# Four attention items in flight and a new order of the early units in a two-layer NSA and HGRN2 decoder kernel

## The reference

```python
def reference(x, ...):
    for i in range(2):
        h = rms_norm(x, norm_w[i])
        y = nsa_mixer(h, ...) if i == 0 else hgrn2_mixer(h, ...)
        x = x + y
    return rms_norm(x, final_norm)

def nsa_mixer(h, w_in, ...):              # 16 heads of 64 in 4 groups
    q, kc, vc, ks, vs, kw, vw, gl, z = split_cols(h @ w_in, ...)
    v_cmp, k_cmp = compress(kv(vc), ...), rope(compress(kv(kc), ...), cmp_end)
    # compressed branch: 15 blocks of keys; selected and window branches: with
    # 256 tokens both see every causal key, each with its own K and V
    o = g0 * attend(q, k_cmp, v_cmp) + g1 * attend(q, ks, vs) + g2 * attend(q, kw, vw)
    return (o * jax.nn.silu(z)) @ w_out

def compress(kv, pe, w1, w2):             # blocks of 32 tokens, stride 16
    return jax.nn.silu((blocks(kv) + pe).reshape(...) @ w1) @ w2

def hgrn2_mixer(h, w_in, lb, g_norm, w_out):
    ...                                   # gated linear recurrence, 8 heads of 128
    return (norm(o) * g_norm * jax.nn.silu(z)) @ w_out
```

## Time and profile before

| what | us |
|---|---|
| median of 3 runs | 358.63 |
| lowest and highest run | 356.74, 360.58 |
| the profiled execution | 356.69 |
| its span, first to last instruction | 354.2 |
| PE busy in the span | 332.1 |
| DVE, ACT, POOL busy | 233.6, 181.8, 89.7 |

### The profile page before, as it was taken

How to read it: one execution, slowest core, us unless ns; L and a number is a source line. 1 busy time by engine, 2 the same in 40 slices (tenths; PEclk the granted TensorE clock), 3 DMA queues, 4 the chain that set the end, 5 groups by cost and what they waited for, 6 DMA issues and landing times.

```text
span 354.2 us, 5694 instructions
## 1 busy us (share of the span) xinstructions
PE 332.1 (94%) x2157; PEld 281.1 (79%) x2157; DVE 233.6 (66%) x396; ACT 181.8 (51%) x372; POOL 89.7 (25%) x83
## 2 busy tenths in 40 slices
PE   8999779999989969789899999999999999999993
PEld 5789577878979945466568878999999999889882
DVE  3884693566657779675634872744485997799942
ACT  4950556455564597775705654836473010067721
POOL 2012003343201134463420010022061575533000
PEclk9999989999999999999999999999999999999999
DMA  7999699542749000420430277671656015001011
GB/s 288 370 200 295 251 305 212 196 135 104 150 91 217 20 1 2 134 103 3 160 138 0 62 265 262 211 264 35 223 220 240 0 49 190 2 0 43 18 60 59
DMA packets 28474, 49.37 MB, mean 139 GB/s; under 512 B 3160, under 2 KB 7648, under 8 KB 28448
## 3 DMA queue, kind: packets, MB, share of 16 engines
q1 hardware_dynamic: 25696, 44.82, 40.6%
q10 hardware_dynamic: 2240, 2.17, 3.1%
q0 software_dynamic: 512, 2.03, 1.6%
HBM read 47.97 MB, written 1.05 MB: 138 GB/s over the span
## 4 chain that ended last, share of the span: by engine, by line
PE 66%; DVE 13%; ACT 8%; DMA 7%; issue 3%; POOL 1%; SPq 1%; DVEq 0%; ACTq 0%
PE bank L611 62%; DMA raw<-in_nsa 7%; DVE w_lo L1103 5%; PE bank L791 2%; ACT w_hi L882 2%; ACT prob L1002 1%; DVE nmax L1311 1%; POOL prob L532 1%; PE bank L711 1%; ACT h_hi L889 1%; DVE prob_t L1323 1%; ACT w_hi L908 1%; PE bank L852 0%; DVE zT L1232 0%; DVE zT L1233 0%
## 5 line engine op out<-in xcount | busy, mean ns | idle before, releaser
L1103 DVE TENSOR_TENSOR w_lo<-raw,w_hi 128x1024 fp32r<-128x1024 f32 (+1 forms) x80 | 93.1, 1207 | 39.8 <-ACT w_hi L882 39.8
L611 PE MATMUL bank<-w_hi,h_hi 128*128 128x512 f32 x192 | 77.0, 407 | 3.0 <-DVE w_lo L1103 2.3
L882 ACT ACTIVATE w_hi<-raw 128x1024 fp32r<-128x1024 f32 (+1 forms) x80 | 72.7, 971 | 12.4 <-DMA raw<-in_nsa 10.5
L611 PE MATMUL bank<-w_lo,h_hi 128*128 128x512 f32 x192 | 75.3, 392 | 0.0
L611 PE MATMUL bank<-w_hi,h_lo 128*128 128x512 f32 x192 | 75.2, 392 | 0.0
L611 PE MATMUL bank<-h_hi,w_hi 128*128 128x256 f32 x224 | 64.0, 286 | 0.3 <-DVE w_lo L1103 0.2
L611 PE MATMUL bank<-h_hi,w_lo 128*128 128x256 f32 x224 | 63.4, 283 | 0.0
L611 PE MATMUL bank<-h_lo,w_hi 128*128 128x256 f32 x224 | 63.4, 283 | 0.0
L611 PEld LDWEIGHTS bank<-w_hi,h_hi 128*128 128x128 f32 x192 | 36.0, 188 | 13.8 <-issue 6.2
L611 PEld LDWEIGHTS bank<-h_hi,w_hi 128*128 128x128 f32 x224 | 42.9, 192 | 0.8 <-DVE w_lo L1103 0.7
L611 PEld LDWEIGHTS bank<-h_lo,w_hi 128*128 128x128 f32 x224 | 43.0, 192 | 0.1
(11 more groups left out here) (195 smaller groups left out, 463.9 us busy)
## 6 DMA issues: line engine op xcount, KB each, us to landing
raw<-in_hg SPq DMA_DIRECT2D x16, 1024.0 KB, 7.0
raw<-in_nsa SPq DMA_DIRECT2D x12, 1024.0 KB, 12.6
raw<-in_nsa_out SPq DMA_DIRECT2D x8, 512.0 KB, 8.2
raw<-in_hg_out SPq DMA_DIRECT2D x4, 1024.0 KB, 7.0
raw<-in_nsa SPq DMA_DIRECT2D x4, 512.0 KB, 6.6
w<-in_w1k SPq DMA_DIRECT2D x2, 1024.0 KB, 11.2
w<-in_w1v ACTq DMA_DIRECT2D x2, 1024.0 KB, 16.8
x_res<-in_x SPq DMA_DIRECT2D x2, 512.0 KB, 5.2
```

The lines of the kernel that those rows point to most:

```text
L611: return nc.tensor.matmul(o, lhsT, rhs, start=start, stop=stop, skip_group_check=True)
L882: m = nc.scalar.activation(dst, src, ACT.Copy)
L1103: m = V.tensor_tensor(lo, src, hi.bitcast(F32), ALU.subtract)
```

## The change

It does the following.

1. `NS` is 4, with score banks 4, 5, 6, 3; `prob` gets a fifth buffer, and `p_ct` is laid over `s_c`. `pt` alternates between banks 7 and 1. `pv` of all four jobs is in bank 0. U_O0 and U_O1 for token block 0 are both in bank 2.
2. z: DVE writes the scaled product to `zT`, ACT takes tanh of half of it into the same PSUM bank, and two steps later DVE makes (tanh + 1) z into `zT` and frees the bank; the factor 0.5 goes into the job's product with `pv`.
3. The compressed branch (`sc`, `scT`, `pcT`) is interleaved with z's slices ahead of the items; the second `cmp2` is moved ahead of `stage` 6. The steps of `lb` that follow its exponential move to layer 2.
4. SP issues the constants, then U_KW, then `wg` and `w1`. `cmp1` 0 goes behind U_KW's first block and `gl` behind its second; `cmp2` 0 goes into U_Q0.
5. `SPREAD`, `BEFORE` and `AMONG` have new numbers, and `LAG` is 4 for U_O0 and U_O1.

```diff
-NS = 3
+NS = 4
+S_BANKS = (4, 5, 6, 3)
+PT_BANKS = (7, 1)
...
+Z_BANKS = (2, 3, 2, 0)
+Z_LAG = 2
...
-BEFORE = (3, 3, 2, 0, 0, 0, 5, 0, 3)
-AMONG = (13, 15, 16, 21, 22, 23)
+BEFORE = (3, 2, 2, 3, 3, 2, 1)
+AMONG = (12, 14, 16, 18, 20, 22)
...
     stage(0)
-    add("cmp1", 0, banks=(6,))
     pa(U_KW, 0, 0)
     stage(1)
+    add("cmp1", 0, banks=(6,))
+    pa(U_KW, 1, 1)
     add("gl", banks=(7,))
     add("cmpT", 0, banks=(6,))
-    pa(U_KW, 1, 1)
     stage(2)
+    pa(U_Q0, 0, 2, range(0, 2))
+    add("cmp2", 0, banks=(6,))
+    pa(U_Q0, 0, 2, range(2, 4))
+    stage(3)
     add("glT", banks=(7,))
-    add("cmp2", 0, banks=(6,))
-    pa(U_Q0, 0, 2)
-    stage(3)
...
+    add("cmp2", 1, banks=(6,))
+    stage(6)
     filler(BEFORE[0])
-    stage(6)
+    add("sc", 0, banks=(7,))
     filler(BEFORE[1])
     stage(7)
+    add("scT", 0, banks=(7,))
     filler(BEFORE[2])
-    add("cmp2", 1, banks=(6,))
-    add("sc", 0, banks=(7,))
+    add("sc", 1, banks=(7,))
     filler(BEFORE[3])
-    add("scT", 0, banks=(7,))
-    add("sc", 1, banks=(7,))
+    add("scT", 1, banks=(7,))
     filler(BEFORE[4])
-    add("s", 0, banks=(4,))
-    add("s", 1, banks=(5,))
+    add("pcT", 0, banks=(7,))
+    add("s", 0, banks=(S_BANKS[0],))
     filler(BEFORE[5])
-    add("scT", 1, banks=(7,))
+    add("pcT", 1, banks=(1,))
+    for n in range(1, NS):
+        add("s", n, banks=(S_BANKS[n],))
     filler(BEFORE[6])
-    add("pcT", 0, banks=(7,))
-    add("s", 2, banks=(6,))
-    filler(BEFORE[7])
-    add("pcT", 1, banks=(1,))
-    filler(BEFORE[8])
     for n in range(NI):
-        add("pt", n, banks=(7,))
+        add("pt", n, banks=(PT_BANKS[n % 2],))
         if n + NS < NI:
-            add("s", n + NS, banks=(4 + n % NS,))
+            add("s", n + NS, banks=(S_BANKS[n % NS],))
         if n >= 2:
             m = n // 2 - 1
-            add("pv", m, n % 2, banks=(PAIR_JOB[m] % 2,))
+            add("pv", m, n % 2, banks=(0,))
         filler(AMONG.count(n))
...
-SPREAD = {U_KW: (3, 3, 4, 5), U_Q0: (0, 2, 3, 3), U_Q1: (3, 3, 8, 13), U_Z0: (0, 6, 7, 7),
-          U_Z1: (1, 2, 4, 11), U_O0: (12, 18, 32, 39), U_O1: (32, 38, 46, 54), V_V0: (0, 0, 0, 2),
+SPREAD = {U_KW: (3, 3, 4, 5), U_Q0: (9, 10, 11, 12), U_Q1: (5, 6, 7, 8), U_Z0: (6, 8, 10, 12),
+          U_Z1: (3, 4, 9, 11), U_O0: (12, 18, 32, 39), U_O1: (32, 38, 46, 54), V_V0: (0, 0, 0, 2),
...
-LAG = 2
+LAG = {U_O0: 4, U_O1: 4}
...
-        p_ct = sb("p_ct", [P, 2, 512], F32, att)
+        p_ct = s_c
...
                 if u == NRAW:
-
-                    sp.dma_start(wg[:], t_in["nsa"][:, NSA_GL:NSA_Z].rearrange("(k p) n -> p k n", p=P)).then_inc(wg_in, 16)
                     for dst, src in CONST_LOADS:
                         sp.dma_start(dst, src).then_inc(const_in, 16)
+                if u == NRAW + 1:
+                    sp.dma_start(wg[:], t_in["nsa"][:, NSA_GL:NSA_Z].rearrange("(k p) n -> p k n", p=P)).then_inc(wg_in, 16)
                     load_w1(sp, "k")
...
-                        held = u == U_Z1 and m2 == 0
-                        nc.scalar.activation(z_rows(r0), ps[:], ACT.Copy if held else ACT.Silu).then_inc(taken(key), 1)
-                        if u == U_Z1 and m2 == 1:
-                            wait_taken(act, ("pb", U_Z1, 0))
-                            nc.scalar.activation(z_rows(r0 - 2), z_rows(r0 - 2), ACT.Silu).then_inc(z_silu, 1)
+                        group = Z_GROUPS.index(key)
+                        act.wait_ge(z_scaled, group + 1)
+                        nc.scalar.activation(ps[:], z_rows(group), ACT.Tanh, scale=0.5).then_inc(z_tanh, 1)
...
-                        V.tensor_tensor(both, both, bc(rs_row, 2, 1), ALU.mult).then_inc(z_scaled, 1)
+                        V.tensor_tensor(both(z_rows(Z_GROUPS.index(key))), both(ps[:]), bc(rs_row, 2, 1), ALU.mult).then_inc(z_scaled, 1)
...
-                        dve.wait_ge(z_silu, 1)
-                        for m2 in range(2):
-                            wait_taken(dve, ("pb", U_Z1, m2))
-                        V.tensor_tensor(zT[half], ps[:].rearrange("p (k s) -> p k s", k=4), zT[half], ALU.mult).then_inc(taken(key), 1)
+                        for zk in Z_GROUPS[2 * gp:2 * gp + 2]:
+                            wait_taken(dve, zk)
+                        V.scalar_tensor_tensor(zT[half], ps[:].rearrange("p (k s) -> p k s", k=4), 0.5, zT[half], ALU.mult,
+                                               ALU.mult).then_inc(taken(key), 1)
...
+                for group, zk in enumerate(Z_GROUPS):
+                    if n == LAST[zk] + Z_LAG:
+                        dve.wait_ge(z_tanh, group + 1)
+                        V.scalar_tensor_tensor(z_rows(group), bk(zk)[:], 1.0, z_rows(group), ALU.add, ALU.mult).then_inc(taken(zk), 1)
```

More of the change, by code:

```diff
@@ L66 @@
 JOB_LAST = [max(m for m in range(NPAIR) if PAIR_JOB[m] == j) for j in range(4)]
+Z_GROUPS = [("pb", u, m2) for u in (U_Z0, U_Z1) for m2 in range(2)]
+Z_BANKS = (2, 3, 2, 0)
+Z_LAG = 2
 Z_ORDER = [(V_Z0, 0), (V_Z1, 0), (V_Z0, 1), (V_Z1, 1)]
 STEPS_L = ["diag"] + LEVELS
-BEFORE = (3, 3, 2, 0, 0, 0, 5, 0, 3)
-AMONG = (13, 15, 16, 21, 22, 23)
+BEFORE = (3, 2, 2, 3, 3, 2, 1)
+AMONG = (12, 14, 16, 18, 20, 22)
 ACT_TURNS = (6, 8, 9, 10, 12, 14, 16, 17, 18, 19, 20, 21)
@@ L133, in schedule @@
     z = [(u, m2, sl) for u in (U_Z0, U_Z1) for m2 in range(2) for sl in range(4)]
-    fill = [(("pb",) + s, 2 + s[1]) for s in z]
-    fill += [(("pa", u, 0, sl), 2 + (u - U_O0)) for u in (U_O0, U_O1) for sl in range(4)]
+    fill = [(("pb",) + s, Z_BANKS[Z_GROUPS.index(("pb",) + s[:2])]) for s in z]
+    fill += [(("pa", u, 0, sl), 2) for u in (U_O0, U_O1) for sl in range(4)]
     def filler(n):
@@ L141, in filler @@
                 add(*step, banks=(bank,))
+    add("cmp2", 1, banks=(6,))
+    stage(6)
     filler(BEFORE[0])
[L144 removed]
+    add("sc", 0, banks=(7,))
     filler(BEFORE[1])
     stage(7)
+    add("scT", 0, banks=(7,))
     filler(BEFORE[2])
[L148 to L150 removed]
+    add("sc", 1, banks=(7,))
     filler(BEFORE[3])
[L152 to L153 removed]
+    add("scT", 1, banks=(7,))
     filler(BEFORE[4])
[L155 to L156 removed]
+    add("pcT", 0, banks=(7,))
+    add("s", 0, banks=(S_BANKS[0],))
     filler(BEFORE[5])
[L158 removed]
+    add("pcT", 1, banks=(1,))
+    for n in range(1, NS):
+        add("s", n, banks=(S_BANKS[n],))
     filler(BEFORE[6])
[L160 to L164 removed]
     for n in range(NI):
[L166 removed]
+        add("pt", n, banks=(PT_BANKS[n % 2],))
         if n + NS < NI:
[L168 removed]
+            add("s", n + NS, banks=(S_BANKS[n % NS],))
         if n >= 2:
             m = n // 2 - 1
[L171 removed]
+            add("pv", m, n % 2, banks=(0,))
         filler(AMONG.count(n))
     for c2 in range(2):
[L174 removed]
+        add("pv", NPAIR - 1, c2, banks=(0,))
     filler(len(fill))
@@ L272, in split_places @@
             places[0].setdefault(n, []).append((u, q))
-            places[1].setdefault(min(used - 1, n + LAG), []).append((u, q))
+            places[1].setdefault(min(used - 1, n + LAG.get(u, 2)), []).append((u, q))
     return places
@@ L451, in program @@
         scaled = sem("scaled")
-        z_silu = sem("z_silu")
+        z_tanh = sem("z_tanh")
         y_hi = sem("y_hi")
@@ L503, in wait_pv, with z_rows @@
                 eng.wait_ge(pv_done, m + 1 - sum(j < m for j in JOB_LAST))
+        def z_rows(group):
+            return zT[:, 2 * group:2 * group + 2].rearrange("p k s -> p (k s)")
         def bc(ap, n, at):
@@ L1295, in _ @@
                         V.tensor_tensor(sc, sc, bc(cst[:, i, 0], NP_, 2), ALU.mult).then_inc(cmp_scaled, 1)
-                        if i == 1:
-                            dve.wait_ge(lb_e, 1)
-                            for ins in (lambda: V.tensor_tensor(lb[:, 0], lb[:, 1], lb[:, 2], ALU.add),
-                                        lambda: V.reciprocal(lb[:, 3], lb[:, 0]),
-                                        lambda: V.tensor_tensor(lb[:, 1:3], lb[:, 1:3], bc(lb[:, 3], 2, 1), ALU.mult),
-                                        lambda: V.tensor_tensor(lb[:, 3], lb[:, 1], lb[:, 2], ALU.add),
-                                        lambda: V.tensor_tensor(lb[:, 4], lb[:, 3], lb[:, 1], ALU.subtract),
-                                        lambda: V.tensor_scalar(lb[:, 5], lb[:, 4], -1.0, 1.0, ALU.mult, ALU.add)):
-                                step_(ins())
-                                settled()
                     elif kind == "s":
@@ L1411, in _ @@
                                 V.tensor_tensor(y4, y4, bc(ostat[:, c, 2, 4 * half:4 * half + 4], P, 2), ALU.mult).then_inc(o_norm, 1)
+                    if key == ("pa", V_V1, 1):
+                        dve.wait_ge(lb_e, 1)
+                        for ins in (lambda: V.tensor_tensor(lb[:, 0], lb[:, 1], lb[:, 2], ALU.add),
+                                    lambda: V.reciprocal(lb[:, 3], lb[:, 0]),
+                                    lambda: V.tensor_tensor(lb[:, 1:3], lb[:, 1:3], bc(lb[:, 3], 2, 1), ALU.mult),
```

(5 more changed lines are left out.)

7 lines of the change are left out of this document (1 added, 6 removed).

## The result

The changed kernel takes 349.45 us (median of 4 runs, 348.04 to 350.67), the kernel before, measured beside it, 359.31 (4 runs, 356.74 to 360.58). The ratio is 0.974, with a 95% interval of 0.970 to 0.978: faster. The profiled execution took 349.11 us with a span of 346.5, against 354.2 before. So the span fell by 7.7 us, where the prediction's sum had 11.5. The medians differ by 9.9. A part of that is the choice of the two profiled executions: the 354.2 of before is as low as the lowest of its 20 later executions (354.2 to 358.3, median 355.5), while the four of the changed kernel had 345.8 to 347.9, median 346.95. By these medians the gain is 8.5. All that follows is reckoned in the spans of the profiled executions, unless it says otherwise; with executions of one kernel 2 us apart, a difference of 1 us between two such spans is only as good as the waits that the timelines show for it.

The account below looks back on a forecast made before the run. PE, busy 332.1 of 354.2 us, was taken as the bound, with 14.1 us of gaps. Terms 6.1 + 1.6 + 0.2 + 3.6 = 11.5 gave 345.2 or, from the median, 347.1; forecast 346.0 us, range 340.0 to 352.5.

Parts of the forecast that it names:

- 0.8 for the fourth score: First items: the fourth `s` placed ahead of the items costs 0.8 us early and returns it at the end.
- Part 1: Early units: loading U_KW earlier closes PE's gaps and ends the low-clock stretch, 6.1 us; bounds 2.3 and 6.5.
- cover for w1k: Early units: w1k lands at about 36 us, `cmp1` 0 is moved to 40.3, so 4 us of cover.
- the rival of a late w1k: Early units: w1k lands after 40.3 us, `cmp1` 0 waits and the clock falls again: 352 us; chance 0.06.
- Part 2: Compressed branch: z slices between its steps cover the DVE and ACT chain, both gaps close, 1.6 us; bounds 0 and 1.6.
- Part 3: z's SiLU: tanh served by the exponential's table, no table load; ACT cost between -2.6 and +7.7 us, low end taken.
- the rival of the tables: Tanh is not in the exponential's table: up to eight loads, 9 us of ACT, 350 us; chance 0.05.
- Part 4: First eight items: goes from latency-bound to DVE-bound, with new waits at bank 0; gain 0.2 us, bounds -1.5 and +3.5.
- Part 5: Other sixteen items: two banks and one more item of distance cover PE's waits; 3.6 of 4.5 us, bounds 1 and 4.5.
- Nearly all gaps close: Rival, whole kernel: all PE gaps and the clock loss go, 14.1 + 1.7 = 15.8 us, to 341; chance 0.15.
- The items give nothing: Rival, items: more bank 0 waits, later items keep half their gaps; only parts 1 and 2 gain, 351 us; chance 0.17.
- Slower: the low clock: Rival, items: bank 0 waits lower the clock throughout; gains gone at 12 us of such work, 364 at 18; chance 0.03.

## Why the prediction was right or wrong

The time came within the range (349.45, 340.0 to 352.5) and the direction was right; the forecast of 346.0 was 3.5 too fast. The sum's miss of 3.8 us (3.0 by the medians of spans) lies nearly all ahead of the items: the first `pt` was to come 6.9 us earlier (6.1 + 1.6 less 0.8 for the fourth score) and came 3.5 earlier.

- **Part 1, early units, 6.1: measured 5.0 alone.** Transfer, cover for w1k and `gl`, and the clock were right: no PE gap to 58.5, no wait at `cmp1` 0 (so the rival of a late w1k fell), no low stretch there. The second block of U_Q0 starts 5.9 us earlier in the changed kernel, whose products start 0.4 late. The step that failed is the silent one that what is won at stage 3 arrives at stage 7. The new `SPREAD` of U_Q1 puts two splits of DVE beside POOL's rope sum, whose 2.05 us of extra length become a wait of 1.0 at `kcT`. The prediction costed every moved instruction of DVE, and none by what it does to POOL. The run with these two splits moved shows it: the sum takes 1.28 and the wait is gone. The loss was already in the trace of the kernel before, where a split starts at 73.74 and the rope sum at 73.90 takes 2.18 us; the prediction did not look there.
- **Part 2, compressed branch, 1.6: measured about nothing.** "Both gaps close" was right: the window from 98.1 to 119.7 has no idle time. What was not asked is what `sc` 0 waits for once it is moved ahead of stage 7: ACT's copies of the queries, behind a staging copy, behind POOL, behind DVE's rope, behind U_Z0's splits. It waits 1.9, which takes back the 1.6. It is a wait that took the place of the one removed, in a place where the prediction looked only at PE's cover for the chain after it. More cover (one run) moved the wait; earlier splits (another) removed it.
- **Part 3, tanh: right.** No table load but one from the first `sc` to the end of the items, nine with SiLU. The rule of the Trainium skill named in the prediction ("ScalarE: Activation LUTs", section "Table sets: the hidden batching unit") agrees with these rows, and the rival of the tables fell.
- **Part 4, first eight items, +0.2: measured -0.4.** The size was right and the waits at bank 0 came where they were predicted, for z's fourth group (2 us taken, 1.25 measured) and at the job's change (1.5 taken, 1.02 measured). The reason was half wrong, so the size is in part luck. "Bound by DVE" at 18.8 to 20.2 us of work: DVE was busy for 16.26 of 19.40 us, not over 90% of it (the sum had three splits and eight copies, the window has two and seven), and two splits less gave 3.3 us for 2.4 of work. The stretch was held up by two splits that stood in the wrong places of both orders: ACT's copy ahead of the exponentials at 120, behind which the first wait stands, and DVE's subtractions ahead of maxima, products and copies for which PE was waiting.
- **Part 5, the other sixteen, 3.6 and 0.8 returned: right.** PE's idle time there fell from 4.5 us to 0.4 (one wait behind the last `pt`), 4.1; from the ninth `pt` to the end the gain is 3.4 + 1.2 = 4.6, against 4.4. The prediction named only the copies as causes; 2.2 us of the gap were waits for POOL's scaling, and waits of that kind come back with three items in flight. Two banks and the fourth item are both needed, as the runs without them show.
- **The rivals.** "Nearly all gaps close" is not what the change does, but nearly what it allows: with eight quarters of splits moved, the gain in span is 354.2 - 340.4 = 13.8 us of this rival's 15.8. "The items give nothing" fell. "Slower: the low clock" has a true core in too small a size: stretches of low clock do appear in the items when waits of about 2 us stand there (three runs), but each was 6.8 us long with PE busy for 5 to 6 us in it, some 2.5 to 3 us of time and not 12.

The miss of the profiled spans, added up: 1.1 in part 1, 1.85 in part 2 (1.6 not gained, and 0.25 that the first `pt` came later still), 0.4 from this execution's later start, 0.6 in the first eight items, less 0.2 in part 5: 3.75, to rounding the 3.8.

## What to carry to other kernels

When an order is written out by hand, look for the long instructions that can stand anywhere (here splits of 0.7 to 1.2 us each, needed many microseconds later) and ask at each chain of short ones what stands ahead of it in the queue of each engine that it crosses; putting eight of them elsewhere was worth 6.1 us here, almost as much as the whole change. For a moved step, walk the chain of its inputs back over all engines: its cover on PE alone says nothing. And a part's worth found by undoing it is not a term of a sum: three parts that were worth 7.4 us one by one gave 4.2 together.
